# Seven fp32 matmuls on constant tiles, placed around the sums of the norm on TensorE at each of seven stage boundaries

## What is computed

```python
def rms_norm(x, g):
    xf = x.astype(jnp.float32)
    y = xf * lax.rsqrt(jnp.mean(xf * xf, axis=-1, keepdims=True) + EPS)
    return (y * g.astype(jnp.float32)).astype(x.dtype)
...
        x = x + g1 * mixed

        h = rms_norm(x, norm2_g[l]) * (1.0 + sc2) + sh2
        u = causal_dwconv(h @ w_up[l], ffn_conv_w[l], ffn_conv_b[l])
```

## Time and profile before

| quantity | value |
|---|---|
| median of 3 runs | 2384.41 us (2382.22 to 2384.76) |
| the profiled execution, its own time | 2384.97 us |
| its span, first to last instruction | 2383.0 us |
| mean granted clock of TensorE | 0.973 |
| TensorE busy with matmuls | 2211.8 us (93%), 17470 records |
| VectorE busy | 1665.6 us (70%) |
| ScalarE busy | 1416.6 us (59%) |
| DMA | 394.64 MB, mean 166 GB/s |

### The profile page before, as it was taken

How to read it: one execution, slowest core, us unless ns; L and a number is a source line. 1 busy time by engine, 2 the same in 40 slices (tenths; PEclk the granted TensorE clock), 3 DMA queues, 4 the chain that set the end, 5 groups by cost and what they waited for, 6 DMA issues and landing times.

```text
span 2383.0 us, 42425 instructions
## 1 busy us (share of the span) xinstructions
PE 2211.8 (93%) x17470; PEld 2101.5 (88%) x17470; DVE 1665.6 (70%) x2998; ACT 1416.6 (59%) x2203; POOL 196.4 (8%) x178
## 2 busy tenths in 40 slices
PE   2989999999999999999899899899999899899999
PEld 2979899989998898999899887698999887798999
DVE  5798778678769887775997573646885574647653
ACT  2577887466546888854654556564554547564542
POOL 0000000022000000000330111000200111000000
PEclk9999999999989999999999999999999999999999
DMA  7455556567755454564455422245465323344553
GB/s 278 165 164 182 171 193 220 182 196 230 237 180 165 163 191 163 194 225 156 151 168 186 141 83 93 93 145 165 151 195 183 119 83 98 107 151 150 186 188 131
DMA packets 110593, 394.64 MB, mean 166 GB/s; under 512 B 12320, under 2 KB 13888, under 8 KB 110272
## 3 DMA queue, kind: packets, MB, share of 16 engines
q1 hardware_dynamic: 96768, 343.47, 44.2%
q0 software_dynamic: 11904, 43.03, 5.6%
q10 hardware_dynamic: 1728, 5.43, 0.6%
HBM read 390.83 MB, written 1.05 MB: 164 GB/s over the span
## 4 chain that ended last, share of the span: by engine, by line
PE 70%; DVE 14%; ACT 10%; issue 3%; DMA 1%; SPq 0%; DVEq 0%; ACTq 0%
PE bank L547 69%; ACT scr L1024 4%; ACT WH L1024 3%; DVE WL L1525 3%; ACT L1013 2%; DVE arena L1589 2%; DMA ring<-in_w 1%; ACT arena L1024 1%; DVE scr L1589 1%; DVE arena L2208 1%; PE bank L618 1%; DVE scr L1778 1%; DVE arena L1703 1%; DVE scr L1765 0%; DVE small L1777 0%
## 5 line engine op out<-in xcount | busy, mean ns | idle before, releaser
L1024 ACT ACTIVATE WH<-ring 128x1024 fp32r<-128x1024 f32 (+1 forms) x638 | 669.8, 1052 | 758.6 <-PE bank L547 734.7
L547 PE MATMUL bank<-HTH,WH 128*128 128x256 f32 x3392 | 987.9, 291 | 49.6 <-DVE scr L1589 13.9
L547 PE MATMUL bank<-HTL,WH 128*128 128x256 f32 x3392 | 970.3, 286 | 0.0
L547 PE MATMUL bank<-HTH,WL 128*128 128x256 f32 x3392 | 969.6, 286 | 0.0
L1525 DVE TENSOR_TENSOR WL<-ring,WH 128x1024 fp32r<-128x1024 f32 (+2 forms) x602 | 729.8, 1220 | 236.2 <-ACT WH L1024 234.5
L547 PEld LDWEIGHTS bank<-HTH,WH 128*128 128x128 f32 x3392 | 658.8, 194 | 65.0 <-issue 58.0
L547 PEld LDWEIGHTS bank<-HTL,WH 128*128 128x128 f32 x3392 | 658.4, 194 | 3.3 <-issue 2.9
L547 PEld LDWEIGHTS bank<-HTH,WL 128*128 128x128 f32 x3392 | 657.6, 194 | 0.0
L1013 ACT ACT_TABLE_LOAD x120 | 154.0, 1283 | 42.0 <-PE bank L547 24.9
L547 PE MATMUL bank<-ff2h,WH 128*128 128x256 f32 x512 | 144.0, 281 | 0.0
L547 PE MATMUL bank<-ff2l,WH 128*128 128x256 f32 x512 | 143.8, 281 | 0.0
(11 more groups left out here) (316 smaller groups left out, 3716.8 us busy)
## 6 DMA issues: line engine op xcount, KB each, us to landing
ring<-in_w SPq DMA_DIRECT2D x620, 512.0 KB, 4.0
arena<-in_wada POOLq DMA_DIRECT2D x80, 512.0 KB, 4.7
ring<-in_w SPq DMA_DIRECT2D x16, 384.0 KB, 4.0
arena<-in_wada SPq DMA_DIRECT2D x8, 512.0 KB, 19.3
arena<-in_wada ACTq DMA_DIRECT2D x8, 512.0 KB, 22.0
ring<-in_w SPq DMA_DIRECT2D x8, 288.0 KB, 2.9
XT<-in_xt SPq DMA_DIRECT2D x1, 1024.0 KB, 9.3
arena<-in_s POOLq DMA_DIRECT2D x4, 256.0 KB, 3.6
```

What stands on the lines that cost most here:

```text
L547: ins = e.matmul(out, a, b, start=(start and i == 0), stop=(stop and i == len(pairs) - 1))
L1024: return e.activation(out, a, func, **kw)
```

## The change

TensorE's `boundary` gets a helper `busy(n)`, which issues n float32 matmuls of the constant tile `ones` (128x128) with the constant tile `tri0` (128x256) into bank 5. Nothing reads what they write, and they wait for no semaphore. At every boundary but the first, two of them stand ahead of the waits for the squares of chunks 6 and 7, and five behind the sums: 7 boundaries x 7 = 49 matmuls.

```diff
+            def busy(n):
+
+                for i in range(n):
+                    mm(bank[5][:, 0:T], [(con("ones"), con("tri0"))])
+
             def boundary(st):
+                if st:
+                    busy(2)
                 for c in (range(8) if st == 0 else (6, 7)):
                     p.wait_ge(norm_scalar("sq", st, c))
                     if c == 0:
                         p.wait_ge(in_cst("in"))
                     sums(c, square_tile(c), st, start=(c == 0))
+                if st:
+                    busy(5)
```

## The result

| | before | changed |
|---|---|---|
| median of the runs beside each other | 2383.94 us (4) | 2371.53 us (4) |
| lowest to highest | 2382.22 to 2384.76 | 2367.55 to 2372.50 |
| the profiled execution: own time, span | 2384.97, 2383.0 us | 2371.44, 2369.5 us |
| mean granted clock | 0.973 | 0.983 |

The ratio is 0.9948, with a 95% interval of 0.9936 to 0.9960: 12.4 us less, faster by 0.5%. In the profiled executions the difference is 13.5 us. Over all executions, those beside the experiments included, the kernel before took 2376.16 to 2385.59 us (52, median 2383.0) and the changed one 2367.28 to 2375.15 us (10, median 2371.5). The medians differ by 11.5 us, and a single execution lies up to 7 us from the median of its kernel, much more than the first three had shown.

A forecast was written before the change was run, and what follows sets the result against it. TensorE, busy 2211.8 of 2383.0 us, was taken as the bound, slowed by half clock behind boundaries. Openings save 14.1 us, less 1.8 us delay: 12.3 us less, forecast 2372.5 us, range 2367.5 to 2379 us.

The forecast's parts named there:

- Openings at full clock: Seven openings of 72 matmuls behind the boundaries: 8.5 us each at clock 1.00, 14.1 us less in all.
- The second working, from the time at half clock: Check on the seven openings: 30.1 us at half clock, each losing 0.45 us, 13.4 us in all.
- The delay of the two fillers: Ahead of stages 1, 3, 5 and 7, two fillers overrun a 0.41 us hole: 4 x 0.44 = 1.8 us more.
- The five are hidden: Behind the sums at all boundaries: 2.13 us of fillers fit the 2.88 us idle time, some 0.9 us to spare.
- The gain is kept: Behind the openings: weights and DMA don't hold TensorE, so a shorter opening moves all that follows one for one.
- 1 to 3 us: Clock falls outside the seven openings, 99 us at half clock, shift places: worth 1 to 3 us either way.
- The clock: Mean granted clock of the whole kernel: up from 0.973 to about 0.979, with 30 us less at 0.50.
- the clock falls all the same: First rival, at the boundaries: the clock still falls; 2386.5 us (chance 0.06) or 2394 us (chance 0.03).
- the fillers delay: First rival's other part: fillers cost 1.8 us (chance 0.06), or also overrun the HTL by up to 8 us (0.03).
- Half of the gain is given back: Rival, behind the openings: late weights or bank, or a clock fall in idle time; 5.3 us less, 2379.5 us, chance 0.11.
- the second half of the first rival: Clock falls while the five fillers run, overrunning the HTL by up to 1.1 us x 7: 2394 us, slower, chance 0.03.

## Why the prediction was right

2372.5 us was forecast, and 2371.53 us measured. The mechanism at the openings is shown. That the total is met so closely is partly luck: a loss of 2.9 us behind two openings, which the sum had put at nothing, was made up by differences at places that the fillers don't touch.

- **Openings at full clock: 14.1 us forecast, 13.4 us measured.** Each took 8.6 us in place of 8.5; the matmuls start 0.119 us apart, not 0.118. The second working, from the time at half clock, had given 13.4 us. Shown: with the five fillers all openings of all profiles ran at 1.00; without the five, and nothing else taken away, five of seven did not. That all seven fall without any fillers rests on the one profile of the kernel before.
- **The delay of the two fillers: 1.8 us forecast, 1.96 us measured** in rows (0.46 to 0.52 us at each of four boundaries), and seen again in the length of stage 2.
- **The five are hidden: right.** 0.6 to 0.7 us of idle time is left behind them. Seven more, 3.0 us of matmuls, cost 1.95 to 2.08 us at each boundary, so 0.9 to 1.0 us of them were hidden, which is the margin of 0.9 us that was forecast.
- **The gain is kept: right for five openings, mostly wrong for two.** Stages 1, 3 and 7 have the same length in both kernels, and stages 2 and 5 are no longer but for the delay. Behind the openings of stages 4 and 6, 4.2 us shorter together, the next unit starts only 1.3 us earlier, because TensorE waits there for ScalarE and the clock falls during the transposes. The prediction had looked at the weights behind an opening, in stage 1, and took it that all that follows moves one for one. In stage 6 nothing of the gain is to be seen at the end: from the start of its opening to the start of the next it is 332.0 us before and 332.1 us after.
- **What the fillers don't account for.** The mechanism's own sum is 13.4 - 2.0 - 2.9 = 8.6 us, and the two profiles differ by 13.5 us. The other 4.9 us lie at places that the fillers don't touch: 2.5 us ahead of the sums of stage 1, 2.1 us in stage 4 behind its transposes, 0.6 us in stage 5, and 0.3 us the other way in stage 6. Of the 2.5 us, 1.5 us are the opening of stage 0, which the change leaves alone: 10.08 us at 0.83 before and 8.61 us at 1.00 after. Profiles of one kernel differ by as much: stage 4 took 320.51 and 323.33 us in two profiles of the kernel with five fillers. I had given this 1 to 3 us, from three executions; ten executions of the changed kernel lie 7.9 us apart. How the 11.5 us between the medians of all executions are made up is not known, because only one profile of the kernel before exists.
- **The clock.** 0.979 was forecast, and 0.983 stands in the changed profile. That the profiled executions differ by more than forecast comes for the most part from which executions they are: 0.973 is the least that any execution of the kernel before had (48 beside the experiments: 0.973 to 0.978, mean 0.975), and the ten of the changed kernel have a mean of 0.982. That is 0.007 more, some 33 us less at half clock, close to the 30 us of the forecast.
- **The rivals.** That the clock falls all the same did not happen at any of 14 boundaries in two profiles; that the fillers delay was right as a term and too small to decide. "Half of the gain is given back" took place at stages 4 and 6, by one of the ways that it names (the clock falls in an idle time behind the opening) and by a wait for ScalarE that it doesn't name: 2.9 of 13.4 us. In the working of the second half of the first rival, 2384.8 + 1.8 + 8 is 2394.6, not 2394; nothing hangs on it.

Whether the four 0.5 us can be had in the time of an execution stays open: the medians of 2370.35 us (10 executions), 2372.1 us (12, five fillers only) and 2371.53 us (10, the changed kernel) don't tell the three apart. No version was shown to beat the changed kernel.

## What to carry to other kernels

An idle time of TensorE ahead of dense work may cost twice: look at the granted clock of the stretch behind it, and compare its duration with the same work at 1.00. Matmuls on constants in the idle time took the second cost away here when they were 256 columns wide, stood behind the last matmul that others wait for, and were no more than the idle time holds; what went beyond that, or over the end of a hole that was too short, was paid. Then look at the next wait behind the faster stretch: where it ends by another engine's own time, as at stages 4 and 6, or where the stage waits for VectorE again and again, as in stage 3, TensorE only waits longer.

## What the runs showed that I had not expected

- Two fillers ahead of the squares alone, with 2.75 to 2.9 us of idle time left behind the sums, went with a clock of 1.00 at two openings of seven, and narrow ones at both places at five of seven. The opening of stage 0, which no version touches and which has 2.93 us of idle time ahead of it, ran at 1.00 in seven of the thirteen profiles and at 0.73 to 0.85 in the other six (9.9 to 11.4 us). Whether a given idle time is followed by a fall is not fixed by its length. The Trainium skill, "TensorE: Matmul & The Clock Gate", Part 1, says that the monitor doesn't reset when a kernel starts, which would make a fall depend on when the idle time comes. The seven and six of stage 0 agree with it but don't test it.
- Three fillers (1.3 us of matmuls) behind the sums did as well as five in one profile: seven of seven openings at 1.00, with 1.58 us of idle time left ahead of stage 1.
- Stage 3 took 202.6 to 202.8 us in every profile with no fillers inside it, except 204.7 us where twelve stand ahead of the opening behind it, at a mean clock of 0.97 or 0.98 in the three shown here, and 203.17 us at 1.00.
- Executions of one kernel on one core differ more than the first three showed: 52 of the kernel before have a range of 9.4 us, 0.4% of the time.
